# First stage of a decoder layer on one core: ScalarE forms shift minus high part, and VectorE the low part of the modulated input in one operation from it

## What is computed

```
mod = silu(c) @ w_ada + b_ada
sh1, sc1, gt1, sh2, sc2, gt2 = split(mod, 6)
h    = rms_norm(x, g_pre_mix) * (1 + sc1) + sh1
proj = h @ w_in
u_lru, u_gate, q, k, v, f_logit = split(proj)
```

## Time and profile before

| | us |
|---|---|
| runs of the kernel | 2103.37 median of 3 (2098.65 to 2104.13) |
| the profiled execution, its own time | 2105.65 |
| its span in the trace | 2103.9 |
| PE busy | 2046.8 |
| VectorE busy | 1611.8 |
| ScalarE busy | 796.3 |
| start of the first stage's first closing sum, and of its last | 28.77 and 146.99 |

### The profile page before, as it was taken

One profiled execution on the slowest core, in us unless ns is written; L12 is line 12 of the kernel. 1 busy time (PEld: TensorE's weight loads), 2 busy tenths in 40 slices (PEclk: granted clock), 3 DMA queues, 4 the chain that ended last, 5 costly groups with the idle time before them and its releaser, 6 DMA issues.

```text
span 2103.9 us, 25251 instructions
## 1 busy us (share of the span) xinstructions
PE 2046.8 (97%) x9073; PEld 1670.8 (79%) x9073; DVE 1611.8 (77%) x1863; ACT 796.3 (38%) x1035; POOL 101.1 (5%) x106
## 2 busy tenths in 40 slices
PE   5999999999999989999999999999999999999998
PEld 4777778788778768888888888888888888888886
DVE  7998597776987887686786876866866867868767
ACT  5324612224553254343343343342433433433433
POOL 2001050000220001000000000000000000000000
PEclk8999999999999999999999999999999999999999
DMA  9975458856437762332332333323223323223334
GB/s 363 390 258 180 140 172 308 280 191 210 139 120 270 267 229 87 121 106 94 110 100 90 110 103 107 100 100 109 100 90 122 105 91 110 100 90 110 107 103 191
DMA packets 181583, 324.58 MB, mean 154 GB/s; under 512 B 12584, under 2 KB 49624, under 8 KB 179216
## 3 DMA queue, kind: packets, MB, share of 16 engines
q1 hardware_dynamic: 173600, 302.08, 42.8%
q0 software_dynamic: 3568, 16.95, 2.2%
q10 hardware_dynamic: 4352, 4.73, 0.6%
HBM read 313.20 MB, written 10.52 MB: 154 GB/s over the span
## 4 chain that ended last, share of the span: by engine, by line
PE 74%; DVE 16%; DMA 4%; ACT 3%; issue 3%; DVEq 0%; SPq 0%; ACTq 0%
PE pair L849 11%; PE pair L851 11%; PE pair L850 11%; PE pair L874 9%; PE pair L876 9%; PE pair L875 9%; DVE acc L1457 4%; DVE w_lo L1429 3%; DMA raw<-in_w_in_dram 2%; PE bank L529 2%; PE bank L530 2%; PE bank L531 2%; PE bank L541 2%; PE bank L542 2%; PE bank L543 2%
## 5 line engine op out<-in xcount | busy, mean ns | idle before, releaser
L1877 DVE TENSOR_TENSOR yg<-yg,pair 128x1024 f32<-128x1024 f32 x240 | 289.8, 1218 | 282.9 <-PE pair L876 282.9
L849 PE MATMUL pair<-h_hi,w_lo 128*128 128x512 f32 x1020 | 397.2, 389 | 0.0
L851 PE MATMUL pair<-h_hi,w_hi 128*128 128x512 f32 x1020 | 396.8, 389 | 0.0
L850 PE MATMUL pair<-h_lo,w_hi 128*128 128x512 f32 x1020 | 396.8, 389 | 0.0
L874 PE MATMUL pair<-w_hi,op_lo 128*128 128x512 f32 x840 | 328.4, 391 | 0.0
L876 PE MATMUL pair<-w_hi,op_hi 128*128 128x512 f32 x840 | 326.9, 389 | 0.0
L875 PE MATMUL pair<-w_lo,op_hi 128*128 128x512 f32 x840 | 326.9, 389 | 0.0
L979 ACT ACTIVATE w_hi<-raw 128x1024 fp32r<-128x1024 f32 (+1 forms) x114 | 118.4, 1044 | 300.4 <-DMA raw<-in_w_in_dram 188.4
L849 PEld LDWEIGHTS pair<-h_hi,w_lo 128*128 128x128 f32 x1020 | 191.4, 188 | 39.9 <-issue 0.2
L851 PEld LDWEIGHTS pair<-h_hi,w_hi 128*128 128x128 f32 x1020 | 191.5, 188 | 39.8
L850 PEld LDWEIGHTS pair<-h_lo,w_hi 128*128 128x128 f32 x1020 | 191.5, 188 | 39.8
(11 more groups left out here) (273 smaller groups left out, 2764.2 us busy)
## 6 DMA issues: line engine op xcount, KB each, us to landing
raw<-in_w_ada_dram SPq DMA_DIRECT2D x128, 512.0 KB, 4.5
w_raw<-in_w_ff_dram SPq DMA_DIRECT2D x128, 512.0 KB, 3.7
raw<-in_w_ff_dram SPq DMA_DIRECT2D x128, 512.0 KB, 4.3
raw<-in_w_in_dram SPq DMA_DIRECT2D x74, 512.0 KB, 4.7
gst<-in_w_ada_dram SPq DMA_DIRECT2D x64, 512.0 KB, 7.9
raw<-in_w_out_dram SPq DMA_DIRECT2D x32, 512.0 KB, 4.9
x_tok<-in_x_dram SPq DMA_DIRECT2D x4, 1024.0 KB, 8.4
xr<-in_x_dram POOLq DMA_DIRECT2D x4, 1024.0 KB, 7.9
```

The costliest lines, as they stand in the source:

```text
L849: pe.matmul(b, lo[:, cols], h_hi[:, kt, :], start=(kt == 0), stop=False)
L850: pe.matmul(b, hi[:, cols], h_lo[:, kt, :], start=False, stop=False)
L851: last = pe.matmul(b, hi[:, cols], h_hi[:, kt, :], start=False, stop=(kt == KT - 1))
L1877: dve.tensor_tensor(y, y, pairs[2 + (i + r) % 2][:, :, :], ALU.subtract if i == 6 else ALU.add).then_inc(product_read, 1)
```

## The change

ScalarE, in the group's loop over its two feature tiles, does two activations instead of one: the high part as before, then, after waiting for it, the rest: shift minus high part, in the float32 tile that held the full value. VectorE does one operation a tile instead of two: xn times A plus the rest, written as the low part. It waits for the rest, and for mod_read as `h_whole` did. The order of everything else is the same.

```diff
-        def h_sum_of(kt):
+        def h_rest_of(kt):
             return x_tok[:, kt // 4, kt % 4 * COLS:(kt % 4 + 1) * COLS]
...
                 for kt in (2 * j, 2 * j + 1):
                     act.activation(h_hi[:, kt, :], xnT[:, kt, :], ACT.Identity, bias=S1[:, kt:kt + 1],
                                    scale=A1[:, kt:kt + 1]).then_inc(h_hi_ready, 1)
+                    act.wait_ge(h_hi_ready, kt + 1)
+                    act.activation(h_rest_of(kt), h_hi[:, kt, :].bitcast(F32), ACT.Identity, bias=S1[:, kt:kt + 1],
+                                   scale=-1.0).then_inc(h_rest, 1)
...
-            def h_whole(kt):
-
+            def h_low(kt):
                 dve.wait_ge(mod_read, kt // 2 + 1)
-                dve.tensor_scalar(h_sum_of(kt), xnT[:, kt, :], A1[:, kt:kt + 1], S1[:, kt:kt + 1],
-                                  ALU.mult, ALU.add).then_inc(h_sum, 1)
-
-            def h_low(kt):
-                dve.wait_ge(h_hi_ready, kt + 1)
-                dve.wait_ge(h_sum, kt + 1)
-                dve.tensor_tensor(h_lo[:, kt, :], h_sum_of(kt), h_hi[:, kt, :].bitcast(F32), ALU.subtract).then_inc(h_lo_ready, 1)
+                dve.wait_ge(h_rest, kt + 1)
+                dve.scalar_tensor_tensor(h_lo[:, kt, :], xnT[:, kt, :], A1[:, kt:kt + 1], h_rest_of(kt),
+                                         ALU.mult, ALU.add).then_inc(h_lo_ready, 1)
...
                 take_start(j)
-                for kt in (2 * j, 2 * j + 1):
-                    h_whole(kt)
                 for kt in (2 * j, 2 * j + 1):
                     h_low(kt)
                 lo_part(Q_UNIT[j])
```

More of the change, by code:

```diff
@@ L255, in hybrid_layer @@
         x_ssq, x_std, x_scaled, xt_done, xt_copied = (sem(n) for n in ("x_ssq", "x_std", "x_scaled", "xt_done", "xt_copied"))
-        h_hi_ready, h_sum, h_lo_ready = (sem(n) for n in ("h_hi_ready", "h_sum", "h_lo_ready"))
+        h_hi_ready, h_rest, h_lo_ready = (sem(n) for n in ("h_hi_ready", "h_rest", "h_lo_ready"))
         u_copied, conv_done, z_done, sig_done = (sem(n) for n in ("u_copied", "conv_done", "z_done", "sig_done"))
```

## The result

The changed kernel takes 2117.42 us, the median of 4 runs (2114.07 to 2118.51); the kernel before takes 2103.68 in 4 runs (2098.65 to 2104.13). The ratio is 1.006, with a 95% interval of 1.0045 to 1.0075: slower by 0.6%, or 13.7 us. The profiled execution took 2118.51 us with a span of 2116.7, against 2105.65 and 2103.9: +12.9 and +12.8.

A forecast was written before the change was run, and what follows sets the result against it. The prediction took VectorE to bound the modulated-input stage up to its last group, then PE. Its terms, 10.7 us from the groups plus 0.1 in the last, gave 2103.37 + 10.8 = 2114.2, forecast 2114, range 2109.5 to 2119 us.

The forecast's parts named there:

- the forecast's own upper bound: Median of the whole kernel: 2117.1 us, from 12.0 us added and 1.7 us for PE's clock.
- The bound: Stage forming the modulated input: VectorE bounds it up to the eighth and last group, PE from there on.
- ScalarE's chain: Each group: high, rest, high, rest on ScalarE, finished 3.04 us after its start instead of 1.52.
- +1.55 us a group: Each group, ScalarE's first high part to the next weights' low part (L1429): 3.72 us instead of 2.17.
- How the groups add up: Groups 0 to 6 each pass on 1.55 us, 10.9 in all; PE's lateness in one absorbs 0.2: 10.7.
- The last group: Eighth group, where PE takes over: at most 0.1 us of PE idle time before the first low part.
- The fall of the clock: PE at 1.2 GHz after idle time and column job: hidden in groups 2 to 6, +1.7 us in the last.
- PE's wait for L1491 grows to about 2.2 us a group: Sign of being right: PE idles about 2.2 us before each group's column job, waiting for VectorE's closing sum.
- The sum: Whole kernel: 10.7 us from the groups plus 0.1 from the last one, +10.8 us.
- VectorE's saving counts: ScalarE's results arrive before VectorE needs them, so eight groups save 6.8 us, to 2098.9 profiled; 3 in 100.
- the shift is absorbed later: A later place sets its own pace, leaving under 6 of the 10.8 us, median some 2106; 1 in 10.
- PE becomes the bound through the clock: Clock falls before most groups, adding 9 us, or 2 to 4 in mild form, up to 2120; 12 in 100.

The follow-up runs named there:

- the second execution: The changed kernel run again, unaltered, beside the kernel before: median 2117.31 us, ratio 1.0056.
- the waits filled: Changed kernel with unit Q's low part and three rows of the next group's sums moved into VectorE's idle time: 2104.06 us, ratio 1.0003 to the kernel before.
- the rest formed but not used: Kernel before plus ScalarE's two added activations, written to a spare tile nobody reads, VectorE keeping its four operations: 2110.15 us, ratio 1.0035.

## Why the prediction was right, point by point

- **The number.** The median of 2117.42 lies in the stated range (2109.5 to 2119), 3.4 us above the forecast of 2114 and 0.3 above the forecast's own upper bound of 2117.1. The mechanism held; four terms were too small or left out, all on the same side.
- **The bound.** Right. VectorE sets the pace through the groups; PE takes over in the last one.
- **ScalarE's chain.** Right to 0.01 us: the rest takes 0.72, it starts 0.04 after the high part, the next high part 0.62 after it, and the last rest ends 3.03 after the start (forecast 3.04).
- **+1.55 us a group.** It was 1.63. The term that was mis-sized is the step from the rest to the low part: 0.10 us instead of 0.02, of which 0.07 go with the wait on mod_read in front of the one that holds, a part of the change that I had costed at nothing. My 0.02 came from the old low part, which has two waits too, but with the holding one first. The new operation's 0.752 us against 0.743 adds 0.01.
- **How the groups add up.** From the first closing sum to the last one it takes 158.67 - 28.98 = 129.69 us against 118.22: +11.47, where 10.7 was said. Seven times 1.63 is 11.41, so the 0.2 us that PE's lateness should have absorbed did not come off in the sum. It did come off in its own group (18.55 against 17.07 us, +1.48), but the period before that one grew by 1.82 (18.72 against 16.90), as in the changed kernel the column job of group 1 ran in part at the low clock and took 1.20 us instead of 1.02.
- **The last group.** Low 0 cost PE 0.3 us, not 0.1. The fall of the clock was named at 1.7 us, given 3 in 10 and left out of the number. It came in both profiled executions of the changed kernel, so the case given 3 in 10 is the one that was measured, and cost 1.3 us; PE had the 0.3 us of waiting to hide a part of it in. The forecast that groups 2 to 6 cover it was right: the period is 18.55 us with and without a fall. The sign "PE's wait for L1491 grows to about 2.2 us a group" came in every other group only (2.02, 0.83, 2.02, 0.85, 1.99 us); that a fall takes away the next idle time was not foreseen.
- **The sum.** In the profiles: +0.21 ahead of the first closing sum (chance: in the second execution it starts at 28.48, 0.29 before that of the kernel before), +11.47 in the groups, 32.02 - 30.41 = +1.61 in the last one, 13.3 us at the first gate matmul, and 12.8 at the end. In the medians +13.7 stands against +10.8, of which the four terms above make 0.6 + 0.2 + 0.2 + 1.3 = 2.3; the rest is within the spread of the runs. (By the recorded ratio, 1.0060, the difference is 12.6 us.)
- **The rivals.** That VectorE's saving counts (3 in 100) fell, as written: its waits ate it. With the waits filled the period is 0.66 us shorter than before. That the shift is absorbed later: behind the first gate matmul the changed kernel takes 1926.0 us and the one before 1926.5, 0.5 of 13.3 us at most. That PE becomes the bound through the clock came in a mild form only.
- **The rule on the number of operations** from the page "VectorE: DVE Perf Modes" of the Trainium skill, section "Rules for kernel authors", holds for VectorE's busy time here (5.8 us less) and not for the kernel's, as each operation saved on one engine had become an activation of a chain on another.

## What to carry to other kernels

Two operations that run beside another engine's work cost less than one that must wait for it: when an operation is fused across engines, count the links from the event that releases both to the last result, not the busy time of either. A saving on the bounding engine becomes a saving of time only when something else of its list stands in the new wait; here that brought +0.6% back to level. And when that engine gets faster, look at who is next: PE, late after a stretch at the low clock, hid most of the gain until it was kept busy there (and one wait was dropped), and only then were 0.2% left.

## What the runs showed of the hardware that was not expected

- A wait on a semaphore long satisfied, in front of the wait that holds a VectorE operation, cost 0.07 us on the path (gap of 0.10 against 0.04). Behind the wait that holds, as in the kernel before and with the rest formed but not used, the gap is 0.02 to 0.03 us with two waits. No run exchanges the order of the same two.
- A column operand in the scalar_tensor_tensor of 512 columns costs 0.06 us of length (0.752 against 0.693 us) and nothing in its start.
- The granted clock fell in every other group of the changed kernel: a fall takes away the idle time that leads to the next one. It fell behind 12 of 15 column jobs with 2.0 us of idle time ahead, and behind 5 of 10 with 1.14 to 1.56 us, so equal cases end both ways. Filled with eight matmuls, the same places showed no fall in any of five groups.
- Behind the stage, where no kernel differs from another, the rest of the layer took 1924.1 to 1926.7 us in fourteen executions. Differences of 1 to 2 us are to be read in the stage, not in the time of the kernel.
